# One word of padding ahead of the rounded weights and their remainders

## The reference, cut to what matters

```
def swiglu(h, w_gate, w_up, w_down):
    return (jax.nn.silu(h @ w_gate) * (h @ w_up)) @ w_down        # 1024 -> 2816 -> 1024, two layers
...
proj = h @ w_in        # 1024 -> 2304, split into two kinds of attention
down = h @ w_down      # latent attention, 1024 -> 672, then 384 -> 1536 and 256 -> 2048
...
proj = xn @ w_in[l]    # 1024 -> 3328: a recurrent mixer (RWKV-7) and differential attention
h = h + rms_norm(mix @ w_out[l], ln_attn_post[l])
u = causal_dwconv(hn @ w_up[l], conv_w[l], conv_b[l])             # 1024 -> 5632, three taps
f = (jax.nn.gelu(gate, approximate=True) * val) @ w_down[l]       # 2816 -> 1024
```

## Time and profile before

| | |
|---|---|
| median of three runs | 1925.72 us |
| the profiled execution: span from the first to the last instruction | 1924.0 us |
| lowest and highest run (no run has a time of its own beside the profile) | 1923.92, 1926.21 us |
| TensorE matmuls (PE), busy | 1890.1 us, 98% of the span |
| TensorE weight loads (PEld), busy | 1527.6 us, 79% |
| VectorE (DVE), ScalarE (ACT), GpSimd (POOL), busy | 52%, 38%, 9% |
| share of the chain that ended last that is TensorE's | 90% |
| mean granted TensorE clock | 0.995 |

### The profile page before, as it was taken

How to read it: one execution, slowest core, us unless ns; L and a number is a source line. 1 busy time by engine, 2 the same in 40 slices (tenths; PEclk the granted TensorE clock), 3 DMA queues, 4 the chain that set the end, 5 groups by cost and what they waited for, 6 DMA issues and landing times.

```text
span 1924.0 us, 26779 instructions
## 1 busy us (share of the span) xinstructions
PE 1890.1 (98%) x10729; PEld 1527.6 (79%) x10729; DVE 999.1 (52%) x1418; ACT 740.1 (38%) x1111; POOL 179.1 (9%) x215
## 2 busy tenths in 40 slices
PE   9999999999999999999999999999999999999998
PEld 7875788888888777788888888777878778888887
DVE  5456453434325686553343434749563566656523
ACT  4247432222224575542222323554342454333322
POOL 1001210000001100010000000303551100000001
PEclk9999999999999999999999999999999999999999
DMA  6310133232322202123223232321120223232321
GB/s 201 105 44 1 50 99 98 87 109 87 105 92 80 72 23 66 45 91 105 91 87 109 88 109 87 100 88 44 24 67 25 88 77 109 87 108 89 107 90 66
DMA packets 137795, 158.74 MB, mean 83 GB/s; under 512 B 15976, under 2 KB 125552, under 8 KB 137712
## 3 DMA queue, kind: packets, MB, share of 16 engines
q1 hardware_dynamic: 136272, 155.01, 25.2%
q0 software_dynamic: 1440, 2.58, 0.5%
HBM read 153.89 MB, written 3.68 MB: 82 GB/s over the span
## 4 chain that ended last, share of the span: by engine, by line
PE 90%; DVE 6%; ACT 2%; issue 1%; DMA 0%; SPq 0%; POOL 0%; ACTq 0%; DVEq 0%
PE bank L2893 35%; PE bank L2926 16%; PE bank L2425 13%; PE bank L2450 3%; PE bank L2980 2%; PE bank L2569 2%; PE bank L2944 2%; PE bank L2839 1%; PE bank L2872 1%; PE bank L2597 1%; PE bank L2688 1%; PE bank L2584 1%; PE bank L2511 1%; PE bank L2541 1%; DVE XL L1589 1%
## 5 line engine op out<-in xcount | busy, mean ns | idle before, releaser
L2893 PE MATMUL bank<-XH,w_hi 128*128 128x512 f32 x992 | 386.8, 390 | 0.7 <-DVE arena L1889 0.7
L2893 PE MATMUL bank<-XL,w_hi 128*128 128x512 f32 x992 | 386.0, 389 | 0.0
L2893 PE MATMUL bank<-XH,w_lo 128*128 128x512 f32 x992 | 385.9, 389 | 0.0
L2893 PEld LDWEIGHTS bank<-XH,w_hi 128*128 128x128 f32 x992 | 186.2, 188 | 39.9 <-DVE arena L1889 0.9
L2893 PEld LDWEIGHTS bank<-XL,w_hi 128*128 128x128 f32 x992 | 186.2, 188 | 39.1 <-issue 0.5
L2893 PEld LDWEIGHTS bank<-XH,w_lo 128*128 128x128 f32 x992 | 186.2, 188 | 38.8
L2425 PE MATMUL bank<-XH,w_hi 128*128 128x512 f32 x448 | 178.7, 399 | 2.5 <-DVE w_lo L1582 2.4
L2425 PE MATMUL bank<-XH,w_lo 128*128 128x512 f32 x448 | 175.3, 391 | 0.0
L2425 PE MATMUL bank<-XL,w_hi 128*128 128x512 f32 x448 | 175.1, 391 | 0.0
L1582 DVE TENSOR_TENSOR w_lo<-w_raw,w_hi 128x2048 fp32r<-128x2048 f32 (+5 forms) x67 | 116.4, 1757 | 93.9 <-ACT w_hi L1036 93.5
L1936 DVE TENSOR_TENSOR w_lo<-w_raw,w_hi 128x2048 fp32r<-128x2048 f32 x24 | 55.0, 2292 | 174.2 <-ACT w_hi L1347 174.2
(11 more groups left out here) (459 smaller groups left out, 3336.1 us busy)
## 6 DMA issues: line engine op xcount, KB each, us to landing
w_raw<-in_ffn_w_gate SPq DMA_DIRECT2D x22, 1024.0 KB, 5.3
w_raw<-in_ffn_w_up SPq DMA_DIRECT2D x22, 1024.0 KB, 5.3
w_raw<-in_ffn_w_down SPq DMA_DIRECT2D x22, 1024.0 KB, 4.9
w_raw<-in_w_up SPq DMA_DIRECT2D x22, 1024.0 KB, 5.1
w_raw<-in_w_in SPq DMA_DIRECT2D x13, 1024.0 KB, 5.3
w_raw<-in_w_down SPq DMA_DIRECT2D x11, 1024.0 KB, 5.0
w_raw<-in_even_w_in SPq DMA_DIRECT2D x8, 1024.0 KB, 5.3
w_raw<-in_even_w_out SPq DMA_DIRECT2D x4, 1024.0 KB, 5.3
```

The costliest lines, as they stand in the source:

```text
L2893: m = pe.matmul(bank[b][:, :], w[:, k, P * c:P * (c + 1)], x[:, k, :], start=(k == 0 and j == 0), stop=(k == KT - 1 and j == 2))
```

## The change

`sb` gets an argument for the alignment, a tensor of one word per partition is put behind `w_raw`, and `w_hi` and `w_lo` are aligned to 4 bytes instead of 32. Nothing else is edited. No instruction is added, taken away or put elsewhere in its engine's order; only addresses differ.

```
-        def sb(name, shape, dt=F32):
-            return ctx.enter_context(nc.sbuf_tensor(name, shape, dt))
+        def sb(name, shape, dt=F32, align=32):
+            return ctx.enter_context(nc.sbuf_tensor(name, shape, dt, align_bytes=align))
...
         w_raw = sb("w_raw", [P, 2, UW])
-        w_hi = sb("w_hi", [P, 2, UW], F32R)
-        w_lo = sb("w_lo", [P, 2, UW], F32R)
+        sb("one_word", [P, 1])
+        w_hi = sb("w_hi", [P, 2, UW], F32R, align=4)
+        w_lo = sb("w_lo", [P, 2, UW], F32R, align=4)
         identR = sb("identR", [P, P], F32R)
```

## The result

The changed kernel takes 1960.5 us (median of 4 runs, 1959.5 to 1961.74) against 1925.47 us for the one before (4 runs beside it): ratio 1.0184, 95% interval 1.0172 to 1.0196. It is 35 us slower. The profiled execution has a span of 1957.7 us, against 1924.0.

The account below looks back on a forecast made before the run. TensorE's distance between matmuls was taken to bound the kernel. The terms 0 + 0.8 + 0 + 0 - 0.7 came to 0, so the span stays at 1924 and the median forecast is 1925.8 us; range 1917 to 1985.

Parts of the forecast that it names:

- no change: Whole kernel: the forecast of 1925.8 us, its own range 1922 to 1929.5; chance 0.47.
- rival (a): TensorE's held and streamed factors at different places within 64 bytes: slower, +5.7 us (1931) or +46 us (1971); chance 0.27.
- What bounds the kernel: TensorE: matmuls fill 98% of the span; one nanosecond more on each of some 5,950 is 6 us.
- Role 1: Weights held, 5,950 loads: one more line, 3.4 ns at most, covered by 30 ns; taken as 0.
- forecast marker: Sign in the changed kernel's weight loads: LDWEIGHTS of 188 ns shows the held-weights step right, over 218 wrong.
- Role 2: Weights streamed, 960 matmuls: one more line, 1.7 ns each, 1.6 us at most; 0.8 in the sum.
- rival (b): Word-off streams fetched at two thirds speed where weights are streamed: +82 us, 2008; loads slowed too, up to +231; chance 0.13.
- the far end: Weights streamed, words fetched in pairs: three fetches for two, 107 ns more per 512-column matmul, 82 us in all.
- Roles 3 and 4: VectorE reading `w_hi` and writing `w_lo`, ScalarE writing `w_hi`: 0 each, ScalarE at most +2.4 us.
- Role 5: `arena` and small tensors 32 bytes later: 216 matmuls get back up to 6.6 ns each, 1.4 us; taken as -0.7.

Follow-up runs that it names:

- e3: Against the kernel before: weights (`w_hi`, `w_lo`) 32 bytes later, tokens (`XH`, `XL`) unmoved; 1962.5 us in one run.
- e7: Against the kernel before: weights 64 bytes later, tokens unmoved; 1960.2 us in one run.
- e8: Against the kernel before: weights 128 bytes later, tokens unmoved; 1958.7 us in one run.
- e2: Against the kernel before: weights 16 bytes later, still on the 16-byte line, tokens unmoved; 1938.4 us, ratio 1.0089.
- e6: Against the kernel before: weights 36 bytes later, so off the 16-byte line, tokens unmoved; 1966.1 us in one run.
- e1: Against the kernel before: tokens and weights both one word off the 16-byte line, at a common place (164); 1990.9 us, ratio 1.0341.
- e5: Against the kernel before: only the tokens one word off (164), weights still at 160; 1987.6 us in one run.
- e11: Against the kernel before: only the tokens two words (8 bytes) off the 16-byte line, weights at 160; 1959.7 us in one run.
- e4: Against the kernel before: only the small tensors and the arena 32 bytes later, weights and tokens unmoved; 1925.8 us in one run.
- e12: Against the kernel before: only `w_lo` one word later (164), `w_hi` and tokens unmoved; 1962.7 us in one run.
- e10: Against the kernel before: weights 256 bytes later, tokens unmoved; 1926.1 us in one run.

## Why the prediction was right and wrong

The measured 1960.5 us lies in the range (1917 to 1985), but its likeliest case, no change, did not come; rival (a) did, at 0.27. The range holds the result only because it was drawn wide enough for that rival: the forecast's own range, 1922 to 1929.5, doesn't. Point by point:

**What bounds the kernel** was right: the distance between matmuls is the whole effect, and one nanosecond on each of some 5,950 is 6 us.

**Role 1, the step that failed.** The prediction looked only at the load's own length and its cover of 30 ns, and took 0. The load did stay at 188 ns, so its forecast marker held, and yet the matmul beside it grew by 5.7 ns. On all of the 5,950 that would be 34 us; of the measured 33.7 some 27 are its share (22.2 in the loops above, the rest in the projections), since the 96 of L2945 stayed at 233.3 ns and smaller groups grew by less. What the runs put in its place: with the held and the streamed factor at the same place modulo 256 bytes and on the line (160 and 192 were tried), TensorE runs at 226.7 ns per matmul of 512 columns. At the other offsets tried it takes about 233 with tokens streamed, on the 16-byte line too (e3, e7, e8), and 16 bytes gives either (e2). The change lost the common place. That it left the 16-byte line isn't what cost, by its neighbours: 32 bytes on the line cost slightly more (e3, 233.3 against 232.4), and 36 bytes, with the load off the line, cost the same in two loops of three (e6). For the 4 bytes themselves the two can't be told apart, since a one-word offset always puts one factor on an odd word.

**Rival (a)** named this mechanism, from the 397 ns of the arena rows, and its two prices bracket the result: 0.8 ns per matmul if cost grows with the offset, 6.6 if any offset costs the whole. It was the second, a little less than whole. Its measure, the place within 64 bytes, was too short: 64 bytes cost as well (e7). The evidence argued for a larger chance than 0.27: one pair of rows with nothing else to explain them stood against an expectation from covers. The argument against it, that one word mostly stays in the same line, had no row.

**Role 2 and rival (b).** A stream one word off does cost, 236.7 ns where the aligned one had 226.7: 10 ns instead of the 1.7 at most that was taken, and far from the 107 of the far end. An aligned stream out of step has 233.4 (e3), so some 6 or 7 of them go with the lost common place and the rest with the odd word; but the two don't simply add, since at a common place an odd stream has 237.8 (e1). In the sum it is 480 x 10 ns = 4.8 us in the last down product and 1.4 in the rows of L2451, 6.2 where 0.8 stood. Pairs of words do matter (e5 against e11), but no stream ran at two thirds of its speed.

**Roles 3 and 4** were right to 2 ns: the neighbours on VectorE and ScalarE that already read and wrote off the line told it.

**Role 5** was wrong in its mechanism and harmless: -0.7 was taken, and L2945 stayed at 233.3 ns. The prediction compared the arena with `XH`, but what meets the arena in these matmuls is the weights, and they moved too: 224 against 164, 60 bytes apart. A place within 64 bytes was also the wrong measure: with the arena 64 bytes from unmoved weights (e4) the first down product has 229.2 or 233.3 ns, not 226.7.

**The pages.** "TensorE: Matmul & The Clock Gate" of the Trainium skill, section "Step-by-step: what each phase is for", says that the weight load takes no read bandwidth from the running matmul. No run here measures bandwidth by itself, but the place of what is loaded does bear on the pace of the matmuls beside it: with loads of unchanged length, moving only what is loaded made the matmuls beside them 5.7 ns longer (changed kernel), and moving one load of three made all three longer (e12). "SBUF — State Buffer" of the Trainium skill, section "Specifications (TRN2)", has lines of 16 bytes and wants two hits or more on each. A stream in pairs of words has these in e11 (8 bytes off) too, and it has the 233.3 ns of aligned kernels; one word off, where every second pair lies across two lines, it has 237.9 (e5). That fits the rule in its direction, but the size is 4.5 ns and not the 107 of rival (b), and no run shows how the words are fetched.

**What stays open.** Why the common place helps isn't shown. The reading that fits is that load and stream share something in memory by address, and that at a common place they settle into a rhythm that avoids each other; for it speak the two rhythms of e2, and e12. A constant length isn't the mark of the fast rhythm: in e3 it is constant too, and slow, as its third matmul of a group shows (min/median/max):

```profile
L2894 PE MATMUL bank<-XH,w_lo x992: 395/396/398, 271.8 to 1829.6; 128*128 128x512 f32 x199
```

No run changed the moment at which a load starts, so this is argued, not shown. Between 16 and 256 bytes the loops were tried only at 32, 36, 64 and 128. That 256 is the period rests on e10 and on the 24 matmuls shown above. Why the direction matters at 64 bytes (228.9 against 233.3), at 8 (230.7 in e11 with the stream below the load, 233.3 above) and perhaps at 16 isn't shown. Nor is it shown why an odd word costs a stream 4.5 ns at one offset (e5) and 1.4 at another (e6).

No version that beats the kernel before came out: 226.7 ns is the lowest distance for 512 columns in any of the fourteen, and moving the arena to the weights' place as well would be worth at most 216 x 6.6 ns = 1.4 us, 0.07%; it wasn't run.

## What to carry to other kernels

Where TensorE is saturated with float32r matmuls of 512 streamed columns, each with a 128x128 load of its own, put the held and the streamed factor at the same place modulo 256 bytes, on a 32-byte boundary as here, all of them: that was worth 1.8 to 2.0% of the time against the even offsets of 32 to 128 bytes, and one of the two weight tensors out of place lost all of it (e12). Keep what is streamed on an even word; VectorE and ScalarE didn't mind. A group of rows whose identical instructions differ by a few nanoseconds with nothing waited for is worth more than an argument from cover: multiply its difference by the count of the main loop before giving it a chance.

## What the runs showed that was not expected

- The same instructions at other addresses: from 226.7 over 232.4 to 233.3 up to 237.9 ns per matmul of 512 streamed columns, up to 66 us of 1925.
- Offsets of 128, 64 and 32 bytes cost 5.7 to 6.6 ns with tokens streamed, 256 bytes nothing. With the streamed factor 64 bytes above the held one it is only 2.2 to 2.5 ns (e7, e4).
- An offset of 16 bytes can give either distance, by layer and by execution (1938 or 1950 us).
- With 256 streamed columns the order is another: 119.8 ns at a common place, 123.0 with the streamed weights one word off, 11.20 / 96 = 116.7 ns in e3, where they are 32 bytes away. What is best for 512 columns isn't best for 256, but 384 x 3 ns is 1 us here.
